# Gated DeltaNet rounds in a 1-core decoder trunk: VectorE's order within a round, the decay on ScalarE, other PSUM banks in the lead-in, side pieces moved

## The reference, cut to what matters

```
g = cumsum(g); decay = where(tril, exp(gdiff), 0)            # gdiff = g_i - g_j
lower = where(strict, (k*beta @ k.T) * decay, 0)
T = triangular_solve(eye + lower, eye)
u, w = T @ (v*beta), T @ (k*beta*exp(g))
intra = (q @ k.T) * decay
step:  v_new = u - w @ S;  o = (q*exp(g)) @ S + intra @ v_new
       S = S * g_last + k_tail.T @ v_new
o = rms_norm(o) * silu(z)                                    # per head
y = gelu(s5); y = y * sigmoid(y @ w_glu)                     # "glu"
out = concat([o, y]) @ w_out                                 # "out0a" (o part), "out0b" (y part)
mod = silu(c) @ ada_w[i] + ada_b[i]                          # "ada": adaLN vectors
```

## Time and profile before

| | us |
|---|---|
| median of 3 runs | 2972.33 (2971.35 to 2974.8) |
| the profiled execution | 2972.34 |
| its span | 2970.7 |
| of it: lead-in of the DeltaNet part | 499.8 to 552.1 |
| rounds 0, 1, 2, 3 begin | 552.1, 642.2, 735.1, 827.2 |
| state chain of round 3, then `out0a` | from 910.9, from 931.1 |
| PE busy, share of the span | 2694.0, 91% |
| DVE busy, ACT busy | 2050.5 (69%), 1207.0 (41%) |

### The profile page before, as it was taken

The page is one execution under the profiler, slowest core; times in us unless marked ns, Lnnn a source line. Parts: engine busy times, 40 slices in busy tenths (PEclk is TensorE's granted clock), DMA queues, the critical chain, the costliest instruction groups (busy, mean ns, idle before and its releaser), DMA issues.

```text
span 2970.7 us, 43497 instructions
## 1 busy us (share of the span) xinstructions
PE 2694.0 (91%) x17100; PEld 2443.7 (82%) x17100; DVE 2050.5 (69%) x2623; ACT 1207.0 (41%) x1572; POOL 235.3 (8%) x290
## 2 busy tenths in 40 slices
PE   1299998778789899999999989999889999999998
PEld 1288887778788688988998889999878898889887
DVE  7778888635645877777777788756887755555556
ACT  0145554322214644334434445355345434443444
POOL 0012222111110000000000101100000000000000
PEclk6589999766768999999999999999899999999998
DMA  9853333334444588888788859945657856555552
GB/s 339 275 185 115 126 115 114 128 128 142 140 144 142 170 284 281 270 279 287 268 276 288 275 175 326 336 152 168 232 171 271 278 185 196 186 185 198 187 194 87
DMA packets 291423, 616.08 MB, mean 207 GB/s; under 512 B 23211, under 2 KB 23746, under 8 KB 291010
## 3 DMA queue, kind: packets, MB, share of 16 engines
q1 hardware_dynamic: 258626, 488.04, 49.5%
q0 software_dynamic: 32640, 125.84, 12.3%
HBM read 611.73 MB, written 2.10 MB: 207 GB/s over the span
## 4 chain that ended last, share of the span: by engine, by line
PE 82%; DVE 9%; issue 4%; ACT 2%; DMA 1%; SPq 1%; POOL 0%; DVEq 0%; ACTq 0%; POOLq 0%
PE groups L2356 12%; PE groups L2360 11%; PE groups L2358 11%; PE groups L2348 11%; PE groups L2352 10%; PE groups L2350 10%; PE pm L1137 2%; PE pc L2526 2%; PE pa L1017 1%; DVE ada_acc L1862 1%; PE pb L2515 1%; PE groups L1002 1%; PE pm L2323 1%; SPq L1521 1%; PE groups L1012 1%
## 5 line engine op out<-in xcount | busy, mean ns | idle before, releaser
L1596 ACT ACTIVATE w_hi<-w_raw 128x1024 fp32r<-128x1024 f32 x776 | 817.3, 1059 | 1232.0 <-PE groups L2360 549.3
L1880 DVE TENSOR_TENSOR w_lo<-w_raw,w_hi 128x1024 fp32r<-128x1024 f32 x749 | 909.1, 1223 | 564.1 <-ACT w_hi L1596 560.2
L2348 PE MATMUL groups<-w_hi,act_hi 128*128 128x512 f32 x1408 | 554.8, 394 | 24.9 <-DVE act_lo L2010 24.9
L2352 PE MATMUL groups<-w_lo,act_hi 128*128 128x512 f32 x1408 | 550.9, 391 | 0.0
L2350 PE MATMUL groups<-w_hi,act_lo 128*128 128x512 f32 x1408 | 550.8, 391 | 0.0
L2356 PE MATMUL groups<-act_hi,w_hi 128*128 128x256 f32 x1776 | 517.7, 292 | 33.6 <-DVE act_lo L2010 13.1
L2358 PE MATMUL groups<-act_lo,w_hi 128*128 128x256 f32 x1776 | 509.8, 287 | 0.0
L2360 PE MATMUL groups<-act_hi,w_lo 128*128 128x256 f32 x1776 | 509.3, 287 | 0.0
L2356 PE MATMUL groups<-hid_hi,w_hi 128*128 128x256 f32 x1392 | 388.1, 279 | 0.0
L2360 PE MATMUL groups<-hid_hi,w_lo 128*128 128x256 f32 x1392 | 386.6, 278 | 0.0
L2358 PE MATMUL groups<-hid_lo,w_hi 128*128 128x256 f32 x1392 | 386.6, 278 | 0.0
(11 more groups left out here) (390 smaller groups left out, 2808.4 us busy)
## 6 DMA issues: line engine op xcount, KB each, us to landing
ada_units<-in_ada_w_dram POOLq DMA_DIRECT2D x120, 1024.0 KB, 6.5
w_raw<-in_ffn_w_gate_dram SPq DMA_DIRECT2D x88, 1024.0 KB, 5.3
w_raw<-in_ffn_w_up_dram SPq DMA_DIRECT2D x88, 1024.0 KB, 5.3
w_raw<-in_ffn_w_down_dram SPq DMA_DIRECT2D x88, 1024.0 KB, 5.3
w_raw<-in_cd_w_in_dram SPq DMA_DIRECT2D x48, 1024.0 KB, 5.7
w_raw<-in_ab_w_in_dram SPq DMA_DIRECT2D x40, 1024.0 KB, 5.1
ada_units<-in_ada_w_dram SPq DMA_DIRECT2D x80, 512.0 KB, 4.6
ada_first<-in_ada_w_dram SPq DMA_DIRECT2D x24, 1024.0 KB, 9.5
```

What stands on the lines that cost most here:

```text
L1596: act.activation(whi[:, half, k], raw[:, slot, k], ACT.Copy).then_inc(hi_done, 1)
L1880: dve.tensor_tensor(wlo[:, half, k], raw[:, slot, k], whi[:, half, k].bitcast(F32), ALU.subtract).then_inc(lo_done, 1)
L2348: pe.matmul(dst, hi[:, k, rows], whi[:, j % 2, kk], start=(k == 0), stop=False, skip_group_check=True)
L2352: last = pe.matmul(dst, hi[:, k, rows], wlo[:, j % 2, kk], start=False, stop=(k == UK * p["units"] - 1), skip_group_check=True)
```

## The change

Seven things change, in the lead-in, the four rounds and the end:

- **VectorE's order in a level.** `intra` (L831 before), which waits for a product of the same level, moves from ahead of level 0's work to behind level 0's additions. The 12 convolution steps go three to each of levels 0 to 3 (before: 2, 3, 3, 4). `norm_qk` moves ahead of level 6's addition, and `lower` of the next round directly behind it, ahead of `takeP`.
- **The decay on ScalarE.** `decay_arg` goes from four VectorE instructions (subtract, minimum) to four ScalarE activations (Relu of gcum minus row, then Exp with scale -1), in level 1, followed there by `rows_b` and by `decay`, which was in level 2. `row_b` no longer waits for it on its own. GpSimd's mask moves from level 3 to level 2.
- **Half of `state_off` on ScalarE.** The scaling of kS (two instructions, L851) becomes `key_state` on ScalarE, at the head of level 3.
- **`DVE_PARTS`** goes from (1, 2, 2, 1, 2, 2, 2) to (2, 2, 1, 1, 2, 2, 2).
- **TensorE in a round.** The even ada tile goes ahead of `power_up`, in level 0 both tiles, with the side piece behind them and ahead of `power_up`. At the end of a round `gram` of the next one goes ahead of `turn_k` and `turn_out`.
- **The lead-in.** Rows go to `pa`, norms to `pb` and `pc`. The second glu group accumulates in `pg[:, 0]`, so its first four pieces (8 to 11) go ahead of `norm_q` and `norm_k`.
- **The end.** `turn_out(3)` goes behind the first unit of `out0a`.

The diff, cut to its core:

```diff
-DVE_PARTS = (1, 2, 2, 1, 2, 2, 2)
+DVE_PARTS = (2, 2, 1, 1, 2, 2, 2)
...
+        bank_g = lambda i: F0 if i else pa[:]
+        bank_q = lambda i: F0 if i else pb[:]
+        bank_k = lambda i: F1 if i else pc[:]
...
+            def decay_arg(i):
+                on(dne, f"gi{i}")
+                if i:
+                    on(dnd, f"at{i - 1}")
+                for p in range(4):
+                    last = act.activation(dcy[:, p], q4(bank_g(i), p), ACT.Relu, scale=-1.0, bias=gate_col(GCUM, p, i))
+                done(last, f"dm{i}")
+
             def decay(i):
-                on(dnd, f"dm{i}")
-                done(act.activation(dcy[:], dcy[:], ACT.Exp), f"ed{i}")
+                on(dna, f"dm{i}")
+                done(act.activation(dcy[:], dcy[:], ACT.Exp, scale=-1.0), f"ed{i}")
...
+            def key_state(i):
+                on(dne, f"kS{i}")
+                for a in range(2):
+                    last = act.activation(kst[:, a], q4(F1, a), ACT.Copy, scale=gate_col(BEG, 2 * a + 1, i))
+                done(last, f"ks{i}")
...
                 for k in range(LEVELS):
+                    if k == 3 and i:
+                        key_state(i - 1)
                     power_copy(i, k)
...
                     if k == 1:
                         if nxt:
+                            decay_arg(i + 1)
                             rows_b(i + 1)
+                            decay(i + 1)
                         if i:
                             take(i - 1, "S", sst, pairs(F1))
-                    if k == 2 and nxt:
-                        decay(i + 1)
...
-                    if k == 0:
-                        intra(i)
-                        if nxt:
-                            convolve(i + 1, range(2))
...
-                    if k == 1 and nxt:
-                        decay_arg(i + 1)
-                        convolve(i + 1, range(2, 5))
-                    if k == 2 and nxt:
-                        convolve(i + 1, range(5, 8))
-                    if k == 3:
-                        if i:
-                            state_off(i - 1)
-                        if nxt:
-                            convolve(i + 1, range(8, 12))
-                            beta_decay(i + 1)
+                    if k == 3 and i:
+                        state_off(i - 1)
+                    if nxt and k < 4:
+                        convolve(i + 1, range(3 * k, 3 * k + 3))
...
+                    if nxt and k == 3:
+                        beta_decay(i + 1)
...
+                    if nxt and k == 6:
+                        norm_qk(i + 1)
                     level(i, k)
+                    if k == 0:
+                        intra(i)
+                if nxt:
+                    lower(i + 1)
...
-                    pe.wait_ge(grp_done, p["g0"] + g + 2)
+                    pe.wait_ge(grp_done, p["g0"] + (g + 2 if p is out0b else 2))
...
             for n in range(1, 8):
                 side(glu, n)
+            for n in range(8, 12):
+                side(glu, n)
             norm_q(0)
             norm_k(0)
-            for n in range(8, 16):
+            for n in range(12, 16):
                 side(glu, n)
             gram(0)
...
                 for k in range(LEVELS):
-                    power_up(i, k)
                     ada_tile(i, 2 * k)
+                    if k == 0:
+                        ada_tile(i, 1)
+                    else:
+                        power_up(i, k)
                     if side_at(i, k) >= 0:
                         side(out0b, side_at(i, k))
                     if k == 0:
+                        power_up(i, k)
                         gram_q(i)
...
-                    ada_tile(i, 2 * k + 1)
+                    if k:
+                        ada_tile(i, 2 * k + 1)
...
+                if nxt:
+                    gram(i + 1)
                 turn_k(i)
                 if i:
                     turn_out(i - 1)
-                if nxt:
-                    gram(i + 1)
                 ada_sums(i)
...
-            turn_out(i)
+            return lambda: turn_out(last_round)
...
+            def after_first(i, j):
+                if j == 0:
+                    turn_last()
+                ln_shift(0, j)
```

More of the change, by code:

```diff
@@ L786, in convolve @@
                     done(last, f"c{i}.{n}")
-            def decay_arg(i):
-                on(dne, f"gi{i}")
-                if i:
-                    on(dnd, f"at{i - 1}")
-                for p in range(4):
-                    last = dve.tensor_scalar(dcy[:, p], q4(F0, p), gate_col(GCUM, p, i), 0.0, ALU.subtract, ALU.min)
-                done(last, f"dm{i}")
             def beta_decay(i):
```

116 lines of the change are left out of this document (49 added, 67 removed).

## The result

The changed kernel takes 2925.17 us (median of 4 runs, 2920.4 to 2929.88), the kernel before took 2971.97 us in the same job (4 runs, 2971.35 to 2974.8). The ratio is 0.9845, 95% interval 0.9833 to 0.9857: 46.8 us less, where 35 were forecast. The profiled execution of the changed kernel took 2929.88 us (span 2928.2), the longest of its four, so the profiles differ by 42.5 us of span and the medians by 46.8.

The account below looks back on a forecast made before the run. The rounds were taken as bound by latency, TensorE and VectorE waiting for each other. 2972.3 less 35.2 us (stalls 17.3, boundaries 0.8, lead-in 5.4, end 0.7, clock 11) gave 2937 us, range 2908 to 2962.

Parts of the forecast that it names:

- the forecast's own case: Whole kernel: a time of 2925 to 2950 us around the forecast of 2937; chance 0.47.
- the clock follows the stalls: Rival: rounds at full clock for 60% of the time, busy time 44 us less, result 2904 us; chance 0.25 (below 2925).
- What bounds the part: Rounds are bound by latency: of 58.6 us TensorE idle, 53.6 us in 13 stalls end with `dn_d`.
- Four stalls without `w_lo`: Rounds, levels without a `w_lo` piece: four stalls behind `dn_d` vanish, 9.9 us gained; bounds 5 to 9.9.
- Nine stalls with `w_lo`: Rounds, levels with a `w_lo` piece: the chain stays, 7.4 of 43.7 us gone; bounds -3 to 12.
- Round boundaries: Between rounds: `gram` and p stop waiting, 2.6 us, less new waits for `pm`; 0.8 us gained, bounds -3 to 2.6.
- Lead-in: Ahead of the rounds: pieces 8 to 11 fill a wait, `w_hi` starts earlier; 5.4 us gained, bounds 2 to 8.
- End: After the rounds: `out0a`'s first unit starts 3.0 us earlier, 2.3 us taken back; 0.7 us gained, bounds -3 to 3.
- The clock, 11 us: Rounds: share at full clock rises from 33% to 39%, busy time 300.2 to 289, 11 us less; bounds +10 to -44.
- The other signs: New profile: `dn_d` stalls about 36 us, no 8 us VectorE waits, no `pm` wait over 1 us a round.
- The queue behind `w_hi` keeps all it has: Rival: stalls behind `w_lo` gain nothing, 12.1 us remain without a better clock, 2960 us; chance 0.17.
- Light work packed together: Rival, slower: `gram`, transposes, sums and two ada tiles in one row keep the clock low, 2987 us; chance 0.06.

Follow-up runs that it names:

- numbers 1 and 2: One call, a level's `w_lo` piece, moved behind the level's additions: on the changed kernel 2879.79 us, on the kernel before 2903.2 us.
- Number 4: Changed kernel with the decay's argument back on VectorE, 2948.41 us; separately, with `intra` back ahead of level 0's work, 2950.13 us.
- number 3: p again ahead of the even ada tile: on the changed kernel 2939.68 us; with `w_lo` behind the additions and `side_out(3)` early 2871.29 us.
- number 8, parts_old: Changed kernel with `DVE_PARTS` back at (1, 2, 2, 1, 2, 2, 2): 2927.43 us.
- number 7, leadin_old: Changed kernel with side pieces 8 to 11 back behind `norm_q` and `norm_k`, the banks staying: 2929.09 us.
- p_first: Changed kernel with p ahead of the even ada tile again, in level 0 also ahead of the side piece and second tile: 2939.68 us.
- number 6: Last transpose ahead of `out0a`'s first unit again, on the changed kernel: 2925.84 us; `side_out(3)` earlier, on the kernel with `w_lo` behind the additions: 2874.17 us.
- before_low: Kernel before with one edit alone, the `w_lo` piece of a level moved behind the level's additions: 2903.2 us.
- low_noreorder: Kernel with `w_lo` behind the additions and `side_out(3)` early, decay's argument back on VectorE and `intra` back ahead of level 0's work: 2896.3 us.
- decay_dve: Changed kernel with the decay's argument of rounds 1 to 3 back on VectorE, at the head of level 1: 2948.41 us.
- intra_first: Changed kernel with `intra` back ahead of level 0's work: 2950.13 us.

## Why the prediction was right in its mechanisms and short in one term

- **Size: in the range, partly by luck.** The median lies 12 us under the forecast of 2937, and 0.2 us inside the forecast's own case (2925 to 2950); one of the four runs, 2920.4, lies in that of "the clock follows the stalls".
- **What bounds the part: right.** Where `dn_d`'s delay was taken away, its stalls went and the time with them (45 and 69 us in numbers 1 and 2).
- **Four stalls without `w_lo`, 9.9 us: right to the row.** None of them is left. Number 4 shows that the decay and `intra` caused three of them: undone, they bring back stalls into levels 1 and 2 of the rounds named. The fourth (692.16 in the earlier trace rows), behind a level 3, wasn't undone by itself, and neither were the three convolution steps a level, `key_state`, `norm_qk` and `lower`, or `gram`'s new place; their shares are argued.
- **Nine stalls with `w_lo`, 7.4 us: direction right, 5.2 measured** (43.7 to 38.5). The tile's 0.86 us is 0.8 (number 3). The ada part that level 0 of rounds 1 and 3 got costs 1.6 us (number 8), so with the tile these stalls grew by 0.9 each. That level 2 loses one at the same time gains nothing against the kernel before, which had no stall there; in the new order it saves the 0.7 of number 8. The one convolution step less in level 3 gave more than priced in round 0 (2.9 where 1.8 stood) and less in round 2 (1.2 where 2.4 stood). The stalls into level 5 of rounds 1 and 3 lost only 0.3 and 0.1 (4.85 to 4.56, 2.55 to 2.49); what takes the tile's 0.8 back there wasn't separated.
- **Round boundaries, 0.8 us gained: 0.8 lost.** The waits for `pm` came as said (1.4 and 0.4 us). But `gram`, which was to lose its 0.92, waits 1.59 into round 2: its input, the normed k, is early enough in round 0 and too late in round 1.
- **Lead-in, 5.4 us: right in size.** The first p was to begin near 547 and begins at 549.0, of which 1.4 is the later start of the part. The four pieces are worth 4.2 us (number 7). Another 3.8 of the 8.0 us in the ledger come from the two ada tiles, which now run while POOL makes the first mask; the 3.3 us of p's wait in p_first are this.
- **End, 0.7 us: nothing measurable.** The working's waits of "about 3.5 and 2.3" are 3.58 and 2.23. Their sum stands against 6.52, and number 6 finds no difference in the time. It was rightly priced low.
- **The clock, 11 us: the term that was mis-sized.** Busy time in the rounds fell by 21.8 us, twice the term. The working took the 0.70 of a quiet stretch as what the rounds could reach, and put them nearly there (39% of the time at full clock, where 0.70 is 40%). The clock of whole rounds now is 0.71, inside the 0.68 to 0.71 that were to show it, and 0.75 to 0.77 with `w_lo` out of the way, so 0.70 was no ceiling. With 0.71 (42%) the working's own formula gives 210 / (0.42 + 0.58 / 1.81) = 284, so 17 us; the other 5 are its step from a mean clock to busy time, and, as leadin_old shows, they are no more than what two executions can differ by. Round 0 shows the same: it was to take near 82 us and takes 72.3, 9.7 of the 17.8 us from busy time (75.0 to 65.3). Against the sum of 35.2, in the two profiles, the clock gave 10.8 more, the lead-in 2.6 more and what follows the part 2.1 more; idle time in the rounds gave 4.3 less, the end 2.7 less, and the part began 1.4 later. That makes 42.3. The other 4 us of the 46.8 are the changed kernel's profiled execution, which was above its median.
- **The other signs.** The stalls behind `dn_d` sum to 38.5 us where about 36 were named, and one of the nine is of 0.41 us where each was to be over 2. No wait for `pm` passes 1 us, and VectorE's waits of 8 us for gate rows or the q product are gone; the waits over 6 us that it has left in the rounds are for `w_hi` (6.1 to 12.6 us).
- **The rivals.** "The queue behind `w_hi` keeps all it has" is refuted by p_first: the tile ahead of p gives 14.5 us. "The clock follows the stalls" had the right mechanism and too large a size for nine remaining stalls: before_low comes to its 2904 us, with busy time of 263 where it had 256. "Light work packed together" would have needed a clock under 0.61, and the four rounds together have 0.67 or more in every kernel here. (Of the row that it names, `gram` and the transposes have 128 moving columns; only the sums and the tiles have one.)

The Trainium skill ("TensorE: Matmul & The Clock Gate", section "Why this matters for your kernels") asks for no long idle gaps between bursts of matmuls. The table agrees in direction: with 10 us idle instead of 59 the same products take 33 to 39 us less. It doesn't agree with the gaps as the only cause, as the last section shows.

## What to carry to other kernels

In an engine's fixed order, look for what stands directly ahead of the instruction that another engine waits for, and ask of each whether its own input is late; one rounding piece that nobody needed yet cost 45 to 69 us here, and moving it alone, in the kernel before, was worth more than seven edits that mostly filled or moved the waits around it. Price a stall of TensorE at more than its length: where the clock falls and rises, 5 us more idle time came with 25 us more in the medians (17 in the profiles), and on a version with `w_lo` behind the additions two such edits together cost 22. An edit that fills a wait (a tile ahead of p) was worth nothing measurable once the wait was gone, so take the cause away first.

## What wasn't expected of the hardware

A stall of 0.41 us is followed by products at half clock just as one of 5.47 us is (p at 580.45 and 634.43 us takes 1.94 us, 1.08 at full clock), and behind the 0.70 us at 746.49 in the earlier trace rows, and behind one of 1.92 us in before_low, p runs at full clock:

```profile
752.86 1.08 PE L1017 MATMUL pa<-dn_d,dn_mb 128*128 128x64 f32 x8 [1.92 <-DVE dn_d L841]
```

So the length of the stall just ahead doesn't say what the clock will be. The clock also falls where no stall stands just ahead. TensorE's timeline of the changed kernel behind the stall at 634.43, in round 1:

```profile
636.91 0.41 PE L992 MATMUL groups<-act_hi,w_hi 128*128 128x256 f32 x1
...
642.56 1.00 PE L1129 MATMUL pm<-c_act,ada_units 128*128 128x1 f32 x8
643.42 0.69 PE L1002 MATMUL groups<-proj 128*128 128x128 f32 x4
643.95 1.15 PE L1129 MATMUL pm<-c_act,ada_units 128*128 128x1 f32 x8
644.97 1.95 PE L1007 MATMUL pa<-dn_d,dn_mb 128*128 128x64 f32 x8
```

The side piece at 636.91 runs at 1.2 GHz, the tile at 642.56 at 2.4, and p at 644.97, which waited for nothing, at 1.2 again. Between them stand a product with 128 moving columns and a second ada tile, and no gap. So the idle time just ahead doesn't account for the rest of the lost clock (0.75 to 0.77 with 10 us of idle time in 272 to 277); whether it goes with the few columns of the tiles and of p, y and x wasn't tried.

The runs of one kernel spread very unevenly: 26 us for low_noreorder, 21 for parts_old, 19 for before_low, but 4 to 5 for decay_dve, intra_first and p_first, and 3 to 8 a job for the kernel before. Stall lengths hardly differ from one profile to the next (5.45 to 5.47 us for the one into level 6 of round 0 in five kernels), and the changed kernel and leadin_old differ by 6.3 us of busy time at a clock of 0.71 and 0.73, with the same order in the rounds and the same stalls. That points to the clock; only one execution of each kernel was profiled, so for the spread within one kernel it isn't shown. For such kernels an edit of under 5 us can be read from the stalls in the profile, and not from the time or from busy time.
